# A four-mixer, two-layer decoder trunk: expert rows by indirect DMA, down products in column groups, weights in whole row blocks

## The reference

```
logits = h @ router                                  # 8 experts
top_vals, top_idx = lax.top_k(logits, 2); gates = softmax(top_vals)
combine = sum(one_hot(top_idx, 8) * gates[..., None], axis=-2)
for e in range(8):
    out = out + combine[..., e:e+1] * ((silu(h @ w1[e]) * (h @ w3[e])) @ w2[e])
```

## Time and profile before

| | |
|---|---|
| median of 3 runs | 1141.82 us (1140.3 to 1143.33) |
| the profiled execution | 1143.13 us, its span 1141.3 us |
| TensorE busy | 1102.5 us (97%) |
| VectorE, ScalarE, GpSimd busy | 285.3, 192.9, 61.4 us |
| read from HBM | 211.67 MB |

### The profile page before, as it was taken

One profiled execution on the slowest core, in us unless ns is written; L12 is line 12 of the kernel. 1 busy time (PEld: TensorE's weight loads), 2 busy tenths in 40 slices (PEclk: granted clock), 3 DMA queues, 4 the chain that ended last, 5 costly groups with the idle time before them and its releaser, 6 DMA issues.

```text
span 1141.3 us, 22432 instructions
## 1 busy us (share of the span) xinstructions
PE 1102.5 (97%) x9790; PEld 837.2 (73%) x9790; DVE 285.3 (25%) x645; ACT 192.9 (17%) x444; POOL 61.4 (5%) x67
## 2 busy tenths in 40 slices
PE   8999999899999999999999969999999999999996
PEld 6887887488888543887789549595949494949592
DVE  4432473500000001233376341020111112021112
ACT  2244231100000001214323011011010111101011
POOL 2000411000000000000312100000000000000000
PEclk8999999999999999999999989999999999999998
DMA  9633101335554445343210256989898989899870
GB/s 325 196 122 105 43 1 38 111 117 160 160 159 167 156 148 155 119 135 109 74 38 1 74 185 203 343 279 351 287 344 289 343 293 323 305 301 332 279 272 37
DMA packets 168650, 213.34 MB, mean 187 GB/s; under 512 B 5120, under 2 KB 151200, under 8 KB 168480
## 3 DMA queue, kind: packets, MB, share of 16 engines
q1 hardware_dynamic: 166032, 210.29, 56.0%
q10 hardware_dynamic: 2576, 2.45, 0.7%
HBM read 211.67 MB, written 1.05 MB: 186 GB/s over the span
## 4 chain that ended last, share of the span: by engine, by line
PE 95%; DVE 3%; issue 1%; ACT 1%; POOL 0%; DMA 0%; DVEq 0%; POOLq 0%; ACTq 0%
PE bank L518 93%; PE bank L523 1%; DVE tok L1434 1%; POOL small L1343 0%; DMA x_sb<-in_x 0%; DVE b_att L1616 0%; DVE b_q L1413 0%; PE bank L1045 0%; DVE x_sb L1410 0%; PE bank L829 0%; ACT tok L1121 0%; DVE small L1425 0%; ACT hT L1133 0%; DVE hT L1410 0%; PE bank L797 0%
## 5 line engine op out<-in xcount | busy, mean ns | idle before, releaser
L518 PE MATMUL bank<-hT,ring 128*128 128x256 f32 (+1 forms) x1184 | 260.3, 382 | 0.0
L518 PEld LDWEIGHTS bank<-hT,ring 128*128 128x128 f32 (+1 forms) x1184 | 223.4, 189 | 36.1 <-issue 2.7
L518 PEld LDWEIGHTS bank<-region_m,ring 128*64 128x64 f32 x4096 | 170.3, 137 | 8.6 <-issue 8.6
L518 PE MATMUL bank<-region_m,ring 128*64 128x96 f32 x4096 | 173.7, 246 | 2.9 <-DVE region_m L1860 1.6
L518 PE MATMUL bank<-ring,region_e 128*96 128x512 f32 (+1 forms) x368 | 160.0, 594 | 0.0
L518 PEld LDWEIGHTS bank<-ring,region_e 128*96 128x96 f32 (+1 forms) x368 | 64.1, 176 | 89.5 <-issue 88.5
L518 PE MATMUL bank<-ring,hT 128*128 128x256 f32 (+1 forms) x448 | 127.8, 442 | 1.4 <-ACT hT L1138 1.4
L518 PE MATMUL bank<-region_e 128*128 128x128 f32 (+2 forms) x512 | 119.2, 384 | 0.0
L1410 DVE TENSOR_TENSOR region_e<-region_f,bank 128x96 f32<-128x96 f32 (+1 forms) x110 | 31.7, 288 | 341.7 <-ACT region_f L1318 198.9
L518 PEld LDWEIGHTS bank<-ring,hT 128*128 128x128 f32 x448 | 84.0, 190 | 35.7 <-issue 25.8
L518 PEld LDWEIGHTS bank<-region_e 128*128 128x128 f32 (+1 forms) x512 | 71.9, 191 | 46.9 <-issue 46.8
(11 more groups left out here) (234 smaller groups left out, 715.0 us busy)
## 6 DMA issues: line engine op xcount, KB each, us to landing
ring<-in_moe_w SPq DMA_DIRECT2D x80, 1024.0 KB, 6.9
region_e<-in_moe_w SPq DMA_DIRECT2D x40, 1024.0 KB, 6.8
ring<-in_ffn_w SPq DMA_DIRECT2D x33, 1024.0 KB, 5.4
ring<-in_w_in SPq DMA_DIRECT2D x22, 1024.0 KB, 5.4
ring<-in_w_out SPq DMA_DIRECT2D x8, 1024.0 KB, 4.9
ring<-in_moe_w SPq DMA_DIRECT2D x16, 512.0 KB, 5.8
region_e<-in_moe_w SPq DMA_DIRECT2D x8, 512.0 KB, 4.0
ring<-in_w_in SPq DMA_DIRECT2D x2, 1088.0 KB, 5.5
```

What stands on the lines that cost most here:

```text
L518: return nc.tensor.matmul(o, lhsT, rhs, start=start, stop=stop, skip_group_check=True)
```

## The change

- Expert weights: w1 and w3 in row blocks (128 rows x 1408 columns, 5632 B a row), 16 transfers; w2 in six transfers as before. All mixer buffers and the ring become one `arena`, which the whole weights of one expert fill in layer 1; each block is reloaded for the next expert as soon as its products are done. Up runs over k outside and over the 11 tiles inside, in banks 0 to 4.
- ScalarE stores h (rows of `tok`) and x in HBM before the loop. GpSimd fetches the next expert's 96 rows of h by indirect DMA, and adds each expert's y (times its gates) to the rows of x by indirect DMA with add. Lists of rows come from a product of `pick` with token numbers and shares (`place_rows`). Eight transposes turn the fetched rows (after eight of the eleven k of down). The first expert is still gathered, and the last one scattered, on TensorE; x is read back in between.
- Down: five products a k, on output partitions 0-63, 64-95, 96-127 (512 columns each), then 0-63 and 64-127 (256 each).
- The mixers' and router's small products in two halves of 64 columns of weights.
- Warm-up: 36 products of 64 x 64.

```diff
+            def expert_row_a(e, k):
+
+                w = t_in["moe_w1" if k % 2 == 0 else "moe_w3"]
+                sp.dma_start(rows_a[:, k, :], w[0, e, (k // 2) * P:(k // 2 + 1) * P, :]).then_inc(a_landed[k], 16)
+
+            def expert_rows_b(e, b):
+                m = min(2, UPC - 2 * b)
+                src = t_in["moe_w2"][0, e].rearrange("(c p) n -> p c n", p=P)[:, 2 * b:2 * b + m, :]
+                sp.dma_start(rows_b[:, 2 * b:2 * b + m, :], src).then_inc(b_landed[b], 16)
...
+                for k in range(ROWS_A):
+                    if k < ROWS_A - 2:
+                        sp.wait_ge(sem("moe_row_used"), i * (KC - 1) + k // 2 + 1)
+                    else:
+                        sp.wait_ge(full[3], nth(i, 3, 1))
+                    expert_row_a((i + 1) % N_EXPERTS, k)
+                for b in range(ROWS_B):
+                    if b < ROWS_B - TAIL:
+                        sp.wait_ge(sem("moe_w2_used"), i * (ROWS_B - TAIL) + b + 1)
+                    else:
+                        sp.wait_ge(full[b + 1], nth(i, b + 1, 1))
+                    expert_rows_b((i + 1) % N_EXPERTS, b)
+            sp.wait_ge(sem("rows_added"), n * N_EXPERTS)
+            for t in range(NT):
+                sp.dma_start(x_sb[:, t, :], x_rows[t * P:(t + 1) * P, :]).then_inc(sem("x_back"), 16)
...
+            def mm_halves(o, lhsT, rhs, start=False, stop=False):
+
+                for q in range(0, P, HALF):
+                    last = mm(o[q:q + HALF, :], lhsT[:, q:q + HALF], rhs, start=start, stop=stop)
+                return last
...
-                            for f, w in enumerate((w1, w3)):
-                                for k in range(KC):
-                                    for q in range(0, P, HALF):
-                                        at = jj * P + q
-                                        last = mm(banks[b][q:q + HALF, f * CAP:(f + 1) * CAP], w[:, k, at:at + HALF],
-                                                  slot_h[:, k, :], start=(f == 0 and k == 0), stop=(k == KC - 1))
-                            last.then_inc(full[b], 1)
-
...
+                def up_tile(place, k, row, j, start):
+
+                    b, at = place
+                    return mm_halves(banks[b][:, at:at + CAP], rows_a[:, row, j * P:(j + 1) * P], slot_h[:, k, :],
+                                     start=start, stop=(k == KC - 1))
+
+                def down_row(k):
+
+                    def product(o, s0, s1, c0, c1):
+                        return mm(o, slot_act[:, k, s0:s1], rows_b[:, k, c0:c1], start=(k == 0), stop=(k == UPC - 1))
+
+                    product(banks[5][0:HALF, :], 0, HALF, 0, 512)
+                    product(banks[5][HALF:CAP, :], HALF, CAP, 0, 512)
+                    product(banks[5][CAP:P, :], HALF, CAP, 512, D)
+                    low = product(banks[6][0:HALF, 0:GW], 0, HALF, 512, 768)
+                    high = product(banks[6][HALF:P, 0:GW], 0, HALF, 768, D)
+                    return low, high
+
+                def place_rows(o):
+
+                    for t in range(NT):
+                        last = mm(o, pick[:, t, :], pair[:, t, :], start=(t == 0), stop=(t == NT - 1))
+                    return last
+
+                def rows_to_slots(b, c0):
+
+                    for c in range(4):
+                        last = nc.tensor.transpose(banks[b][:, c * CAP:(c + 1) * CAP],
+                                                   slot_rows[:, (c0 + c) * P:(c0 + c + 1) * P], ident[0:CAP, 0:CAP])
+                    return last
 
                 pe.wait_ge(sem("passes_ready"), 1)
+                wait_open(pe, "IX", l)
+                fills(place_rows(bank("IX", l)[0:CAP, 0:2]), "IX", l)
                 n_passes = pe.value_load(passes_i[0:1, 0:1], min_val=1, max_val=MAX_PASSES)
                 with pe.Fori(0, n_passes * N_EXPERTS) as i:
+                    pe.wait_ge(free[7], nth(i, 7, 0))
...
+                    for k in range(KC):
+                        if k == KC // 2:
+                            pe.wait_ge(sem("picks"), i + 2)
+                            place_rows(banks[7][0:CAP, 0:2]).then_inc(full[7], 1)
+                        pe.wait_ge(a_landed[2 * k], 16 * i + 16)
+                        for j in range(5):
+                            last = up_tile(GATE[j], k, 2 * k, j, k == 0 and j == 0)
+                        if k == KC - 1:
...
+                    for k2 in range(ROWS_B):
+                        pe.wait_ge(b_landed[k2], 16 * i + 16)
+                        if k2 == 0:
+                            pe.wait_ge(free[2], nth(i, 2, 1))
+                        elif k2 == 2:
+                            pe.wait_ge(free[3], nth(i, 3, 1))
+                        elif k2 == 5:
+                            pe.wait_ge(free[4], nth(i, 4, 1))
+                        if k2 == ROWS_B - TAIL:
+
+                            pe.wait_ge(free[7], nth(i, 7, 1))
+                            pe.wait_ge(sem("gathered"), 16 * i + 16)
+                            rows_to_slots(7, 0).then_inc(full[7], 1)
+                            pe.wait_ge(free[0], nth(i, 0, 1))
+                            rows_to_slots(0, 4).then_inc(full[0], 1)
+                        for k in range(2 * k2, min(2 * k2 + 2, UPC)):
+                            low, high = down_row(k)
+                        if k2 < ROWS_B - TAIL:
+                            high.then_inc(sem("moe_w2_used"), 1)
+                    low.then_inc(full[5], 1)
+                    high.then_inc(full[6], 1)
+
...
+                n = n_passes * N_EXPERTS
+                for t in range(NT):
+                    last = nc.tensor.transpose(banks[1][0:CAP, t * P:(t + 1) * P], placed[:, t, :], ident)
+                last.then_inc(sem("placed_flipped"), 1)
+                pe.wait_ge(sem("placed_back"), 1)
+                pe.wait_ge(free[5], nth(n, 5, 0))
+                pe.wait_ge(free[6], nth(n, 6, 0))
+                for b, t, half in SCATTER:
+                    mm(banks[b][:, :], placed_t[:, t, :], slot_y[:, half * 512:(half + 1) * 512],
+                       start=True, stop=True).then_inc(sem("last_sums"), 1)
...
-                mm(banks[5][:, 0:256], hT[:, 0, 0:P], hT[:, 0, :], start=True, stop=True)
+                mm(banks[5][0:HALF, 0:HALF], hT[:, 0, 0:HALF], hT[:, 0, 0:HALF], start=True, stop=True)
...
+                        for b in (0, 1):
+                            act.wait_ge(full[b], nth(i, b, 1))
+                            nc.scalar.activation(slot_silu[:, 5 * b:5 * b + 5, :],
+                                                 banks[b][:, 0:5 * CAP].rearrange("p (c s) -> p c s", c=5),
+                                                 ACT.Silu).then_inc(free[b], 1)
+                        act.wait_ge(full[4], nth(i, 4, 1))
+                        nc.scalar.activation(slot_silu[:, 10, :], banks[4][:, 0:CAP],
+                                             ACT.Silu).then_inc(sem("moe_silu"), 1)
+                        act.wait_ge(full[7], nth(i, 7, 2))
+                        for c in range(4):
+                            last = slots_in(c, 7)
+                        last.then_inc(free[7], 1)
+                        act.wait_ge(full[5], nth(i, 5, 1))
                         act.wait_ge(full[6], nth(i, 6, 1))
-                        for c in range(4):
-                            last = slots_in(c, 6)
...
+            def fetch_rows(i):
+
+                pool.wait_ge(free[7], nth(i, 7, 1))
+                pool.sem_inc(sem("fetches"), 1)
+                g.indirect_dma_start(slot_rows, None, h_rows, bass.IndirectOffsetOnAxis(rows_in[:, 0:1], 0)).then_inc(
+                    sem("gathered"), 16)
+
+            with pool.Fori(0, n * N_EXPERTS - 1) as i:
+                fetch_rows(i)
+                pool.wait_ge(free[5], nth(i, 5, 1))
+                pool.wait_ge(free[6], nth(i, 6, 1))
+                pool.sem_inc(sem("scatters"), 1)
+                g.indirect_dma_start(x_rows, bass.IndirectOffsetOnAxis(rows_out[:, 0:1], 0), slot_y, None,
+                                     compute_op=ALU.add).then_inc(sem("scattered"), 16)
+                pool.wait_ge(sem("scattered"), 16 * i + 16)
+                pool.sem_inc(sem("rows_added"), 1)
+            fetch_rows(n * N_EXPERTS - 1)
...
+                        dve.wait_ge(sem("rows_added"), i + 1)
                         dve.wait_ge(full[7], nth(i, 7, 1))
+                        v.tensor_copy(rows_out[:, :], rows_next[:, :])
+                        v.tensor_copy(gate_now[:, :], gate_next[:, :]).then_inc(sem("rows_moved"), 1)
+                        dve.wait_ge(sem("rows_moved"), i + 1)
+                        next_rows(banks[7][0:CAP, 0:2]).then_inc(free[7], 1)
+                        dve.wait_ge(sem("moe_silu"), i + 1)
+                        tt(slot_act[:, 10, :], slot_silu[:, 10, :], banks[4][:, CAP:2 * CAP],
+                           ALU.mult).then_inc(free[4], 1)
+                        for b in (0, 1):
```

(67 more changed lines are left out.)

306 lines of the change are left out of this document (146 added, 160 removed).

## The result

| | before | changed |
|---|---|---|
| median of 4 runs each (range), us | 1141.12 (1140.3 to 1143.33) | 1155.53 (1154.59 to 1157.81) |
| profiled execution: time, span, us | 1143.13, 1141.3 | 1157.81, 1156.0 |
| period of the expert loop, us | 55.08 | 57.32 |
| start of the loop in the span, us | 689.28 | 678.33 |
| end of the loop's last product to end of the span, us | 9.6 | 15.6 |

The ratio is 1.0126, 95% interval 1.0104 to 1.0148. I had forecast 1068 (1050 to 1125); rival A, the price of two widths, had said 1152.

The account below looks back on a forecast made before the run. TensorE bounds the loop, with transfers close behind; period 55.08 to 46.7 us saves 67.0, the end adds 3.7 and 2.2, mixer halves save 11, router 1.5: 1141.3 becomes 1067.7 us of span, forecast 1068 (1050 to 1125).

Parts of the forecast that it names:

- rival A: Down: two widths don't run together and each change empties TensorE; 2.35 us a k, period 57.2, time 1152 us; chance 0.13.
- The step that failed: Down in column groups: products on disjoint groups run together, so down takes 14.2 us plus 0.15 against 19.0, -4.7 a period.
- rows 8: Earlier trace rows at 37.31 us: instructions on rows 0-63 and 64-127 start in pairs within 10 ns, read as separate queues.
- What leaves TensorE: Expert loop: gather, scatter and weight transposes go (-6.88 us), fetched-row transposes and list products come; net -5.1 us a period.
- list: Expert loop: two products on TensorE that make the next list of rows, taken to cost 0.6 us a period.
- Row blocks and indirect transfers: Loop transfers: longer rows at 401 GB/s take 43.1 us, fetch and adding scatter 2.9 more, 46.1 us a period, otherwise hidden.
- B: Rival on weight transfers: long rows no faster than 1 KB rows; period 53.3 us, time 1121 us; chance 0.11.
- C: Rival on the loop's indirect transfers: they are late, at 43 us costing 5 us a period; time 1108 us; chance 0.05.
- Halves and router: Ahead of the loop: small mixer products split in halves save 11 us (0 to 16), the router's products 1.5.
- D: Rival on the mixer halves: they bring nothing because changes of width eat the gain; time 1080 us; chance 0.08.
- Warm-up: Kernel start: shorter small products replace the old warm-up; any half-clock transposes would be hidden; 0 us, between -1 and +3.
- The end: After the loop: last scatter stays on TensorE, +3.7 us, and y's rows are copied out after all of down, +2.2.

Follow-up runs that it names:

- e2: Changed kernel with down in nine products a k, all 32 columns wide, instead of five: 1117.95 us, ratio 0.976.
- e3: Changed kernel with the same five down products sorted by width over each two k's: 1142.74 us, ratio 0.9995, period 55.82 us.
- e1: Changed kernel with down as before the change, two products a k of 96 columns of weights: 1091.29 us, ratio 0.955.
- e13: Kernel before with both the mixer and router products in halves and the warm-up of 36 small products: 1132.91 us, ratio 0.990.
- e5: Kernel before with only the mixer and router products in halves of 64 columns: 1178.97 us, ratio 1.031.
- e6: Kernel before with only the warm-up changed, to 36 products of 64x64 from 10 of 256 columns: 1171.56 us, ratio 1.025.
- e10: e1 with each 512-column down product written as four of 128 columns: 1141.35 us, ratio 0.9985 to the changed kernel.
- e14: Changed kernel with eight of eleven k's of down in nine 32-wide products, the others 96-wide, and 27 warm-up products: 1069.89 us, ratio 0.936.
- e4: Kernel before with only its down products replaced by the change's five, in banks 2 and 3: 1259.38 us, ratio 1.102.
- e11: e2 with 3 of the 11 up and gate column blocks as whole 128-column products: 1201.29 us, ratio 1.050 to the changed kernel.

## Why the prediction was wrong

- **The step that failed** is "If products on disjoint groups run together, k costs (512+256)/1024 of before, 1.29 us". It is true of one width (1.29 us measured in e2) and false of 64 beside 32: 2.42 us. The rows it rested on the earlier trace rows show pairs of equal width only, and those of rows 8 are on disjoint rows, not columns. I had written that no row showed two widths, cited the Trainium skill's rule against it (TensorEngine Tiling (Array Packing), Key Properties; the trace of the changed kernel agrees, with 2.42 us a k), worked its price out within 3%, and gave it 0.13. The rule spoke of exactly what was new in the edit and nothing measured spoke against it; it deserved the larger chance.
- **Rival A** had 2.35 us a k, a period of 57.2 and 1152; measured 2.42, 57.32 and 1155.5. Each change of width is 0.136 us in the changed kernel and 0.15 by e3, not 0.1.
- **What leaves TensorE** held: transposes 0.81 (1.2 forecast), list 0.43 (0.6), no wait at the start of the down (0.3). e1 shows the whole effect, 55.08 to 49.49 us.
- **Row blocks and indirect transfers** held: 395 to 400 GB/s, 46.5 us a period possible (46.1 forecast), fetch and scatter hidden. B and C are out.
- **Halves and router**, -12.5 forecast: the loop starts 10.95 us earlier, and e13 gains 10.7, both with the warm-up in it; D is out. In e5, alone, the loop starts 14.2 us earlier, but the refetches hide it in the time.
- **Warm-up**, 0 forecast (-1 to +3): the first projection starts at 13.8 us for 14.8. That the old warm-up began at the level of 1.2 GHz I had read from durations alone; the granted clock of both stretches is 1.00.
- **The end**, +5.9 forecast, +6.0 measured, in part by luck: the copies take 2.2 as forecast, the scatter's products 4.55 us (in part at half clock) for 3.7, and the tail behind them is 0.8 shorter.
- **Not in the forecast at all**: that the loop's place among TensorE's instructions matters. The change kept it within seven groups (36 + 1686), so nothing of it is in the result; but a forecast of an edit that moves the loop's start as e5 and e6 do, or of nine products for every k (e2), missed by 32 to 53 us.

Still open: why e6 refetches in every second period only, why e10's waits are short and many, and part of e13's forecast. Its loop starts 10.3 us earlier than before, where e5's and e6's starts had promised 15.6; 2.5 us of the difference lie at the start, where TensorE's second group of transposes starts at 14.4 us in e13, 11.9 in e5 and 12.8 before.

## What to carry to other kernels

Pack column groups with products of one width; a product of another width runs alone and pays about 0.14 us at each change. Before judging an edit of a long TensorE loop, look for instruction packets in the DMA view of the loop and for "issue" waits in its chain: they say that the loop no longer stays loaded, and some hundred instructions more or less ahead of it (104 in e6) or in it can be worth 30 us. Where a written rule names the very hazard that an edit is the first to meet, and no row speaks against it, a forecast should not give it one chance in eight.

## What the runs showed of the hardware

- A loop of TensorE within seven groups of 256 instructions (up to 1778, e14) stays loaded; one that reaches an eighth is fetched again, in each iteration (e2, e4, e5, e10) or in every second (e6). In e2, e4, e5 and e6 that is one wait of 3 to 5 us at the loop's turn, then a granted clock of 0.50 for 3 to 6 us, often with shorter waits behind it; in e10 mostly several waits of 0.4 to 2.5 us.
- 64-wide and 32-wide products on disjoint column groups did not overlap in any k looked at (2.42 us a k, where one width takes 1.29); a change of width costs 0.136 to 0.15 us. Among halves, a product of 128 columns of weights by 96 takes 0.39 us, its two halves 0.17 (e11).
- An indirect fetch of 96 rows of 4 KB takes GpSimd 0.93 us to issue and lands after 8.6 us (median). In e14, with the DMA engines at 400 GB/s over the whole period, TensorE waited for neither it nor the scatter.
